# Hybrid decoder block on eight cores: inputs stored by load, a shorter rotary table, sliding attention in rounds of two with projection and gate products between scores and values

## What is computed

```python
mod = silu(c) @ ada_w + ada_b                      # sh1, sc1, ga1, sh2, sc2, ga2
h = rmsnorm(x, ln_mix_g) * (1 + sc1) + sh1
q_lat, kv_lat, k_rope, q_s, k_s, v_s, gl_a, gl_b = split(h @ w_in)
# MLA: 8 heads, 64 + 32 rotary dims, causal over all 4096 keys
q = rmsnorm(q_lat) @ w_uq; k_nope, v = rmsnorm(kv_lat) @ w_ukv; rope on q_pe and k_rope
y_mla = softmax(causal(q_nope.k_nope + q_pe.k_pe) * 96**-0.5) @ v
# sliding: 16 heads, 2 kv heads, window 128 (this block and the one before), bias, sink
y_swa = softmax([q_s.k_s/8 + bias, sink])[:-1] @ v_s
merged = sigmoid(gl_a + b) * (y_mla @ w_o_mla) + sigmoid(gl_b + b) * (y_swa @ w_o_swa)
x = x + ga1 * (merged @ w_o)
h = rmsnorm(x, ln_mlp_g) * (1 + sc2) + sh2
x = x + ga2 * (square(relu(h @ w_ff1)) @ w_ff2)
out = rmsnorm(x, ln_final_g)
```

## Time and profile before

| what | us |
|---|---|
| median of three executions | 1395.92 |
| profiled execution, all cores | 1395.63 |
| span of its slowest core (6) | 1394.0 |
| spans of the eight cores | 1389.4 to 1394.0 |
| TensorE busy by the records | 1283.1 |
| DVE, ACT, POOL busy | 632.3, 655.7, 201.4 |

### The profile page before, as it was taken

The page is one execution under the profiler, slowest core; times in us unless marked ns, Lnnn a source line. Parts: engine busy times, 40 slices in busy tenths (PEclk is TensorE's granted clock), DMA queues, the critical chain, the costliest instruction groups (busy, mean ns, idle before and its releaser), DMA issues.

```text
span 1394.0 us, 20354 instructions; the slowest of 8 cores (1389.4 to 1394.0 us)
## 1 busy us (share of the span) xinstructions
PE 1283.1 (92%) x7010; PEld 587.4 (42%) x7010; DVE 632.3 (45%) x860; ACT 655.7 (47%) x901; POOL 201.4 (14%) x174
## 2 busy tenths in 40 slices
PE   0778889999999899999999999999999999999996
PEld 0533444444444353232444444444444444444442
DVE  2578665666662114324222222664443443443356
ACT  0387778979889716849322222443003103202333
POOL 3000435220035101000233322010000000000000
PEclk9999899999999999999999999999999999999999
DMA  9982754130353205020442524386214204000014
GB/s 168 215 110 41 152 119 102 46 62 1 61 73 86 40 1 54 1 27 1 130 44 27 54 31 61 122 115 98 31 14 78 31 1 79 13 1 1 1 61 181
DMA packets 95250, 88.20 MB, mean 63 GB/s; under 512 B 36768, under 2 KB 79824, under 8 KB 95056
## 3 DMA queue, kind: packets, MB, share of 16 engines
q0 software_dynamic: 72640, 51.03, 27.3%
q1 hardware_dynamic: 22512, 35.89, 8.0%
HBM read 127.15 MB, written 8.41 MB: 97 GB/s over the span
## 4 chain that ended last, share of the span: by engine, by line
PE 81%; ACT 7%; issue 4%; DVE 3%; DMA 3%; SPq 1%; ACTq 0%; DVEq 0%; POOL 0%; another core or an unknown queue 0%; POOLq 0%
PE psb L452 81%; ACT arena L457 7%; DMA arena<-eoh 1%; SPq L275 1%; DVE arena L461 1%; DMA scr<-arena 1%; DVE arena L477 1%; DVE arena L473 1%; DMA arena<-xo 1%; DVE arena L469 0%; DVE arena L466 0%; ACTq L314 0%; DVEq L314 0%; ACT L457 0%; POOL arena L461 0%
## 5 line engine op out<-in xcount | busy, mean ns | idle before, releaser
L452 PE MATMUL psb<-arena 128*128 128x512 bf16 (+7 forms) x7010 | 1283.1, 343 | 99.9 <-ACT arena L457 34.4
L452 PEld LDWEIGHTS psb<-arena 128*128 128x128 bf16 (+4 forms) x7010 | 587.4, 100 | 795.3 <-issue 265.6
L457 ACT ACTIVATE arena<-psb 128x1024 bf16<-128x1024 f32 (+5 forms) x479 | 370.6, 822 | 124.5 <-PE psb L452 121.5
L457 ACT ACTIVATE arena<-psb,arena 128x512 f32<-128x512 f32 x220 | 150.7, 687 | 461.5 <-PE psb L452 396.1
L461 DVE TENSOR_TENSOR arena<-psb,arena 128x512 f32<-128x512 f32 (+4 forms) x228 | 148.0, 661 | 321.9 <-ACT arena L457 217.2
L461 DVE TENSOR_TENSOR arena<-arena 128x512 bf16<-128x512 f32 (+2 forms) x176 | 128.9, 732 | 143.7 <-ACT arena L457 136.3
L457 ACT ACTIVATE arena<-arena 128x512 f32<-128x512 f32 (+3 forms) x196 | 137.9, 716 | 104.6 <-DVE arena L473 69.6
L473 DVE SCALAR_TENSOR_TENSOR arena<-psb,arena 128x512 f32<-128x512 f32 x160 | 120.2, 751 | 138.7 <-PE psb L452 137.9
L477 DVE CAST arena<-psb 64x512 bf16<-64x512 f32 (+1 forms) x126 | 86.8, 689 | 119.4 <-PE psb L452 117.9
L461 POOL TENSOR_TENSOR arena<-arena 128x512 bf16<-128x512 f32 (+1 forms) x56 | 97.5, 1741 | 200.5 <-DVE arena L461 185.9
L473 DVE SCALAR_TENSOR_TENSOR arena<-arena 128x512 bf16<-128x512 f32 (+5 forms) x106 | 80.8, 769 | 4.4 <-ACT arena L457 1.8
(11 more groups left out here) (14 smaller groups left out, 28.9 us busy)
## 6 DMA issues: line engine op xcount, KB each, us to landing
arena<-w_ff POOLq DMA_DIRECT2D x16, 1024.0 KB, 12.0
arena<-ada_w POOLq DMA_DIRECT2D x12, 1024.0 KB, 14.3
arena<-xo SPq DMA_DIRECT2D x16, 512.0 KB, 4.2
arena<-xo SPq DMA_DIRECT2D x4, 2048.0 KB, 9.3
out<-arena SPq DMA_DIRECT2D x16, 512.0 KB, 2.8
arena<-xo POOLq DMA_DIRECT2D x4, 1024.0 KB, 32.3
arena<-xs POOLq DMA_DIRECT2D x4, 1024.0 KB, 32.5
arena<-xs SPq DMA_DIRECT2D x8, 512.0 KB, 4.2
```

The source lines that it names most:

```text
L452: S.op("pe", lambda e: e.matmul(out, lhsT=lhsT, rhs=rhs, start=start, stop=stop), reads=R, writes=Wr, sig=sig, cost=cost_of("pe", out, lhsT))
L457: S.op("act", lambda e: e.activation(out=out, in_=in_, func=func, **kw), reads=R, writes=Wr, cost=cost_of("act", out))
```

## The change

Four things change.

- **Storage.** The host stores x, `ada_w`, the input projection, merge, output and MLP weights and the output so that one load is one contiguous run per partition (16 KB of float32 in most), in place of runs of 512 to 4096 bytes. The four transfers of a merge piece become one, the neighbours' blocks of x have an input of their own (`xhalo`). The first converting loads stand in another order: `ada_w` pieces 2 and 3, x group 0, pieces 0 and 1, x groups 1 to 3.
- **Rotary part.** One angle reduction serves both tables (11 operations on VectorE over 1024 columns, 22 before). Queries keep the products with cosine and sine side by side in 64 rows, and the rotated key stands twice, so that the score matmul, now over 128 rows, adds them: `qr_build` has two operations on VectorE in place of four, and a key group two in place of three, with three more small copies by SP. Half of the squares of an own group go from ScalarE to VectorE.
- **Sliding attention in rounds.** A round takes both key blocks of a query block: four scores, four biases, then one projection tile of half 1 (rounds 0 to 15) or one of 12 gate products of the merge (rounds 16 to 27), then values and sums of the round before. One bank (6) takes the sums, bank 7 the tile between. The merge reads those 12 gate products from SBUF (`graw`) and has 96 matmuls less.
- **Costs and places.** The list schedule counts transfers as faster and tiny matmuls as cheaper; `late_loads` is at head 7 in place of 6, with the neighbours' steps closer together; `Arena.solve` may try more placements.

```diff
-            own = tasks[i]["cost"] + tasks[i]["bytes"] / 180e3
+            own = tasks[i]["cost"] + tasks[i]["bytes"] / (190e3 if tasks[i]["e"] == "pool" else 370e3)
...
-        for i in range(4):
-            S.dma("pool", ada0[i], kc_src(adaw_d, 512 * i, 512 * i + 512), ("ada0", i), writes=[("ada0", i)])
+        for i in (2, 3):
+            ada0_load(i)
...
-        for i in range(NXB):
+        x_load(0)
+        for i in (0, 1):
+            ada0_load(i)
+        for i in range(1, NXB):
             x_load(i)
...
-            tt("dve", rt1[HA, :], PS(pb)[HA, :], tabO[HA, cs], ALU.mult, [("ps", pb), ("tabO", 0)], ["rt1"])
-            tt("dve", rt2[HA, :], PS(pb)[HB, :], tabO[HB, cs], ALU.mult, [("ps", pb), ("tabO", 1)], ["rt2"])
-            for e in range(2):
+            for e, hs in ((0, HA), (1, HB)):
                 qt, qk = q_tile(j, e)
-                rs_ = slice(32 * e, 32 * e + 32)
-                tt("dve", qt[R2, cs], rt1[rs_, :], rt2[rs_, :], ALU.add, ["rt1", "rt2"], [qk + (g, 1)])
+                tt("dve", qt[HB, cs], PS(pb)[hs, :], tabO[hs, cs], ALU.mult, [("ps", pb), ("tabO", 0), ("tabO", 1)],
+                   [qk + (g, 1)])
...
+            for (e, p0) in ((0, 96), (1, 64), (1, 96)):
+                S.dma("sp", Kb[0][e][p0:p0 + 32, ks], Kb[0][0][R2, ks], ("kdup", G), reads=[("Kpe0", 0, G)],
+                      writes=[("Kdup0", G)], group=True)
...
+        for r in range(34):
+            if r < 32:
+                swa_scores(r)
+                if r >= 2:
+                    swa_scale(r - 2)
+                if r < 16:
+                    qs_tile(1, r % 4, r // 4, 7, "dve")
+                    if r == 15:
+                        RING.release(PI_QS[1])
+                elif r < 28:
+                    q = r - 16
+                    gate_tile(q // 8, q % 4, q // 4 % 2)
+            else:
+                swa_scale(r - 2)
+            if 1 <= r <= 32:
+                swa_values(r - 1)
+                swa_sum(r - 1)
...
-                for kc in range(8):
-                    mm(PS(pbase)[:, :], wga[:, kc, :], ho[:, kc, cs], kc == 0, kc == 7,
-                       [slot_key(s), ("ho", g, kc)], [("ps", pbase)])
-                for kc in range(8):
-                    mm(PS(pbase + 1)[:, :], wgb[:, kc, :], ho[:, kc, cs], kc == 0, kc == 7,
-                       [slot_key(s), ("ho", g, kc)], [("ps", pbase + 1)])
+                for x, w in ((0, wga), (1, wgb)):
+                    for kc in range(8):
+                        if 2 * m + x >= 3:
+                            mm(PS(pbase + x)[:, :], w[:, kc, :], ho[:, kc, cs], kc == 0, kc == 7,
+                               [slot_key(s), ("ho", g, kc)], [("ps", pbase + x)])
```

397 lines of the change are left out of this document (205 added, 192 removed).

## The result

The changed kernel took 1415.7 us (median of seven executions; 1396.3 for the kernel before beside it). In three of the seven the cores of a die ran slower as a whole, and the ratio is taken from the other four, 1403.8 to 1415.7 us. It is 1.010, 95% interval 1.006 to 1.014: about 1% slower, where 3.4% faster was forecast. The profiled execution took 1413.48 us. Its slowest cores, 6 and 7 (1411.9 and 1411.2 us), show a mean clock of 0.967; the other six take 1396.6 to 1405.0 at 0.979 to 0.986.

A forecast was written before the change was run, and what follows sets the result against it. The prediction took TensorE, with 81% of the chain of waits, as the main bound, though not in start and latents. 1395.6 - 37 (start and latents) - 4 (MLA) - 7 (sliding attention and merge) = 1348 us; range 1330 to 1374.

The forecast's parts named there:

- Start and latents: Stage before MLA: faster loads and a new order end it near 110 us in place of 147.4, 37 us less.
- 5.3 MB at 214 GB/s, 25 us: Start: group 0's inputs land by 27 us, and the first ones-matmul starts near 30 us, not 56.
- Before group 0 can be worked on: Start: two ada_w pieces, group 0 (3 MB together) and SP's positions and latent weights (2.3 MB) must land first.
- Three engines with 60 to 66 us and one chain: Latents: engine work sets the stage; 78 us at 85% of TensorE's time, plus 2 for the last group's chain.
- The last load is not in the way: Latents: buffers come free as groups are done, and the eighth megabyte of x lands by 75 us.
- 4.9 us, 214 GB/s, as the near row: Start: 16 KB runs land 4.9 us apart, as w_ff2 pieces of 4 KB runs did; other end 7.1 us.
- Rival 2: Start: loads no faster, only their order helps; gain 22 us there, 1363 us in all; chance 0.2.
- On a queue that has nothing else to do but `ho_load`: Latents: SP's 24 more copies of 0.5 us each stand on a queue with only `ho_load` behind them.
- MLA: MLA stage: half of TensorE's 8.3 us of waits for VectorE's casts goes, 4 us less; ends 0 and 8.
- Sliding attention and merge: Sliding attention to merge: rounds of 4.38 us and a shorter merge, 317 against 324 us, 7 us less.
- Rivals 3 and 4: Sliding rounds: 3, tile waits for own round's cast, 1375 us, chance 0.13; 4, no overlap, 1435 us, chance 0.05.
- Projections: Before sliding attention: no gain or cost, as TensorE goes on at 0.216 us a matmul and faster loads were hidden.

The follow-up runs named there:

- e1: Changed kernel with SP's small loads ahead of positions and latent weights, and POOL's first converting load held until gains and hv landed; ratio to before 0.998.
- e3: Changed kernel with ada_w and x stored in 2 KB runs, 1024 packets a load in place of 128; ratio to before 0.995.
- e4: Changed kernel with small inputs packed into one transfer, relT and eoh into a second, both first in SP's queue; ratio to before 0.995.
- k0: Changed kernel with ada_w pieces 0 and 1 ahead of 2 and 3, and x group 0 behind all four; 1399.9 us, ratio to before 1.003.
- h0: e5 with converting loads in the order of the kernel before: ada_w pieces 0 to 3, then x groups; ratio to before 0.988.
- k1: e5 with tq, the scaled query latents, in 4 KB of its own off the memory of rtab; 1373.2 us, ratio to before 0.983.
- h2: e5 with h0's order, divided table copies, new scheduler transfer costs, later merge gate products, and wukv and wuq directly behind w_lat; ratio to before 0.981.
- g2: e5 with only x group 0 loaded, the other seven groups working on the same buffer; ratio to before 0.977.
- e5: e4 with the bias table wtab kept in memory of its own up to phase 1; ratio to before 0.995.
- g1: e5 with the rotary tables filled by two VectorE memsets in place of the twelve copies; ratio to before 0.984.
- e6: e5 with the twelve rotary table copies issued by ScalarE in place of SP; ratio to before 0.990.
- r_norounds: Changed kernel with sliding attention, second half of the query projection and the merge as in the kernel before; ratio to before 1.015.

## Why the prediction was wrong

- **Start and latents, 37 us less forecast, 21.5 more measured.** This term carries 58.5 of the 59.4 us by which the core median missed the forecast. Its first two steps below are what failed in the changed kernel itself; the others show once the inputs come early.
  - *"3 MB and SP's positions and latent weights, 5.3 MB at 214 GB/s, 25 us"*. It counted bytes for both queues together. Group 0 did land at 28.3 us, where 27 was forecast. But SP's queue is served by packets, and the change made POOL's some seven times as long and left the number of SP's small ones alone: `w_lat` landed at 43.4 us, and `eoh`, which the step left out, at 54.2, with every TensorE product behind it: the first 512-column matmul came at 68.5 in place of 30. Shown by e1, e3 and e4, which bring it to 36 to 41.
  - *"Before group 0 can be worked on, two ada_w pieces, the group itself ... must land"*. The latents' biases need the other two pieces, and no group's keys get done without them. With `eoh` late and these products behind group 0's latents the last bias moved from 71.9 to 95.7 us; their place alone is 17 of these 24 us (k0: 78.7), and gives nothing at MLA's start, as group 0 then comes later. Shown by h0: 19 us with the order alone, once the queue is short; k1 shows that 14.5 of them can be had by the memory of `tq` too, which let the table copies into the same chain.
  - *"Three engines with 60 to 66 us and one chain will not do better than 88%; I take 85%: 78 us"*. With early inputs and early biases (h0 to h2) it takes 83 to 90 us from the first matmul; without loads of x, 63 us from the last bias (g2), 69 to 77 with them. The estimate, 80 us with the 2 of the last group's chain, was 3 to 10 us low, and its start was the wrong event.
  - *"The last load is not in the way: ... the eighth megabyte of x lands by 75 us"*. It landed at 132.1 us in the changed kernel, as loads wait for buffers and these for the groups. g2 prices all loads of x behind the first at 21 us of e5's start, 12 of them by the biases.
  - *"4.9 us, 214 GB/s, as the near row"*. In the changed kernel converting loads landed 5.6 to 10.6 us apart at the start, and six MLP pieces of 16 KB runs in a row at 953.9, 961.3, 967.6, 974.2, 980.6 and 986.4: 5.8 to 7.4. The `w_ff2` row was no law of run length. Rival 2 held this, with the order's help as its other half, and the order was the harm. (The "7 to 9 us" a megabyte that it counts with is 9.4 and 9.3 in the two differences that the earlier trace rows give for x.)
  - *"On a queue that has nothing else to do but `ho_load`"*: where the inputs come early, SP's queue held the twelve table copies, 2.3 us apart beside POOL's loads (e4: 40.5 to 65.9), with `wukv`, `wuq` and the store to `scr` behind them. g1 prices them at 16 us, k1 shows that most of it was their source's memory. In the changed kernel they came behind POOL's loads, 0.8 us apart, and cost little.
- **MLA, 4 less forecast.** From its first to its last exponential, core by core, the median is 327.2 us before, 323.0 to 325.5 in e1 to e6 and r_norounds, and 327.5 in the changed kernel, where cores 6 and 7 took 341 at a lower clock and the other six 325.1 to 327.6. So it gained 0 to 2 us there and 2 to 4 in the experiments. TensorE's waits for VectorE's casts, of which half the 8.3 us were to go, fell by 1.6 (8.3 to 6.7 us, core 4): the term is within its bounds and too large.
- **Sliding attention and merge, 7 less forecast**: 7.7 (388.6 to 380.9). Right, and so were the period of the rounds, with the wait for bank 7, ScalarE's pause and the stall. Rivals 3 and 4 fell with the period, 4.36 us on average.
- **Projections, nothing forecast** ("TensorE goes on at 0.216 there"): 4 us less, as it had two waits and a stretch at the lower level there before. **Behind the merge, nothing**: 470 us in both.

Taken together, between the medians of the cores at each mark: 21.5 + 1.7 (MLA, 328.4 to 330.1, with the two slow cores in it) - 4.1 - 7.7 = 11.4 us, and 1402.2 less 1390.8 is 11.4.

The side of the result was not covered: all rivals slower than before lay in the rounds. The warning line "wrong if the group's inputs come early but the stage ends past 120" named the outcome and the chain, but put no price on it.

## What to carry to other kernels

Price a queue by its packets, not its bytes: before making one queue's packets larger, list what small loads another queue has at that time, and pack them or issue them first. When a load's place in a queue changes, follow every reader of it to the first thing that all later work waits for; the first matmul's start is no measure of a stage. Undo suspected causes singly and together: here, at MLA's start, the queue was worth 13 us alone (e5), the order of the pieces nothing (k0), and both 32 (h0). When a scheduler makes the order, look whether an edit changed it, before the gain is put down to the edit. Where an instruction waits for a transfer it doesn't read from, look at what else lies on its memory.
